# A decoder step on one Trainium2 core: one written order for projections, prompt attention and cached attention

## The reference

```python
x = x + 0.5 * swiglu_ffn(x, ffn1)                      # 1024 -> 2 x 2816 -> 1024
u, q, k, v, qm = split(rmsnorm(x) @ w_in)              # 256 | 512 | 512 | 512 | 256
y_pool = pool_mixer(u)                                 # windows 2, 4, 8, 16; 64x64 maps
q, k   = rotary(rmsnorm(q)), rotary(rmsnorm(k))        # 8 heads x 64
y_moba = moba_attention(q, k_all, v_all)               # prompt: causal in one block of 256
                                                       # sample: 3 of 4 past blocks + own key
y_mem  = mem_attention(rmsnorm(qm), mk, mv)            # 4 heads, 256 memory tokens
x = x + concat(y_pool, y_moba, y_mem) @ w_out
x = x + 0.5 * swiglu_ffn(x, ffn2)
```

## Time and profile before

| | us |
|---|---|
| three runs: median (lowest to highest) | 693.55 (693.41 to 695.11) |
| the profiled execution, its own time | 694.32 |
| its span, first to last instruction | 692.5 |
| PE busy, share of the span | 631.7, 91% |
| DVE busy | 383.8, 55% |
| ACT busy | 281.2, 41% |
| POOL busy | 21.3, 3% |
| mean granted clock of TensorE | 0.956 |

### The profile page before, as it was taken

One profiled execution on the slowest core, in us unless ns is written; L12 is line 12 of the kernel. 1 busy time (PEld: TensorE's weight loads), 2 busy tenths in 40 slices (PEclk: granted clock), 3 DMA queues, 4 the chain that ended last, 5 costly groups with the idle time before them and its releaser, 6 DMA issues.

```text
span 692.5 us, 13430 instructions
## 1 busy us (share of the span) xinstructions
PE 631.7 (91%) x5076; PEld 570.1 (82%) x5076; DVE 383.8 (55%) x648; ACT 281.2 (41%) x448; POOL 21.3 (3%) x25
## 2 busy tenths in 40 slices
PE   6799999999999799988995677699899999999997
PEld 4799999998999676666773455479799999999997
DVE  4567777776544556356336323224776766775443
ACT  5633453336333434242335322433634443334331
POOL 1000000000000100000000220000400000000000
PEclk9989999999999999999998857799999999999999
DMA  9967767855874315655745658515455565556531
GB/s 286 256 197 237 228 184 233 239 184 203 284 238 171 106 45 167 215 183 183 254 167 196 208 183 276 166 48 167 128 154 165 178 180 168 168 180 224 178 115 63
DMA packets 132700, 128.18 MB, mean 185 GB/s; under 512 B 6648, under 2 KB 103815, under 8 KB 132655
## 3 DMA queue, kind: packets, MB, share of 16 engines
q1 hardware_dynamic: 132375, 127.60, 58.0%
q10 hardware_dynamic: 288, 0.08, 0.1%
HBM read 124.95 MB, written 2.83 MB: 185 GB/s over the span
## 4 chain that ended last, share of the span: by engine, by line
PE 60%; DVE 16%; ACT 10%; issue 8%; SPq 3%; POOL 1%; DMA 1%; DVEq 1%; ACTq 0%; POOLq 0%
PE banks L1170 16%; PE banks L1171 16%; PE banks L1172 15%; PE banks L1178 6%; ACT w_hi L546 4%; DVE w_lo L839 4%; PE banks L1510 2%; DVE h_tmp L876 1%; PE banks L1273 1%; DVE h_tmp L879 1%; ACT kv L566 1%; DVE sg L871 1%; POOL kv L528 1%; PE banks L1460 1%; SPq L358 1%
## 5 line engine op out<-in xcount | busy, mean ns | idle before, releaser
L839 DVE TENSOR_TENSOR w_lo<-raw,w_hi 128x1024 fp32r<-128x1024 f32 x160 | 196.1, 1232 | 147.0 <-ACT w_hi L546 145.9
L1170 PE MATMUL banks<-x_hi,w_hi 128*128 128x264 f32 x768 | 222.3, 289 | 10.6 <-DVE h_tmp L876 7.6
L1171 PE MATMUL banks<-x_lo,w_hi 128*128 128x264 f32 x768 | 220.5, 287 | 0.0
L1172 PE MATMUL banks<-x_hi,w_lo 128*128 128x264 f32 x768 | 220.2, 287 | 0.0
L546 ACT ACTIVATE w_hi<-raw 128x1024 fp32r<-128x1024 f32 x160 | 164.6, 1051 | 82.8 <-PE banks L1172 80.2
L1170 PEld LDWEIGHTS banks<-x_hi,w_hi 128*128 128x128 f32 x768 | 147.6, 192 | 12.6 <-DVE w_lo L839 9.7
L1171 PEld LDWEIGHTS banks<-x_lo,w_hi 128*128 128x128 f32 x768 | 147.8, 192 | 0.0
L1172 PEld LDWEIGHTS banks<-x_hi,w_lo 128*128 128x128 f32 x768 | 146.9, 191 | 0.0
L1170 PE MATMUL banks<-h_hi,w_hi 128*128 (+1 forms) x352 | 100.2, 285 | 0.8 <-DVE h_tmp L876 0.7
L1172 PE MATMUL banks<-h_hi,w_lo 128*128 (+1 forms) x352 | 100.2, 285 | 0.0
L1171 PE MATMUL banks<-h_lo,w_hi 128*128 (+1 forms) x352 | 100.0, 284 | 0.0
(11 more groups left out here) (233 smaller groups left out, 558.2 us busy)
## 6 DMA issues: line engine op xcount, KB each, us to landing
raw<-in_ffn_w_in SPq DMA_DIRECT2D x88, 512.0 KB, 3.9
raw<-in_ffn_w_out SPq DMA_DIRECT2D x44, 512.0 KB, 3.3
kv<-in_cache_k SPq DMA_DIRECT2D x64, 256.0 KB, 3.5
kv<-in_cache_v SPq DMA_DIRECT2D x64, 256.0 KB, 4.2
raw<-in_w_in SPq DMA_DIRECT2D x12, 512.0 KB, 3.1
raw<-in_w_out SPq DMA_DIRECT2D x8, 512.0 KB, 5.6
raw<-in_mem_w_kv SPq DMA_DIRECT2D x4, 512.0 KB, 3.2
raw<-in_w_in SPq DMA_DIRECT2D x8, 256.0 KB, 3.7
```

The costliest lines, as they stand in the source:

```text
L839: vec.tensor_tensor(w_lo[:, n % RING, :], raw[:, n % RING, :], w_hi[:, n % RING, :].bitcast(F32), ALU.subtract).then_inc(lo_ready, 1)
L1170: pe.matmul(out, lhs[0], rhs[0], start=start, stop=False)
L1171: pe.matmul(out, lhs[0], rhs[1], start=False, stop=False)
L1172: return pe.matmul(out, lhs[1], rhs[0], start=False, stop=stop)
```

## The change: what it does

It puts the whole stage between the feed-forwards into one list, `steps()`, that all engines follow. In it:

1. The column sums come after the sample parts of units 0 and 1; units 2 and 3 follow them.
2. The cached keys are transposed in rounds 1 to 4 and 6 to 9, eight pages a round (`K_PAGES_AT`), one or two pages behind each part; the logits follow in rounds 2 to 5 and 7 to 10, behind the second part (`LOGITS_AT`). Rounds 10 to 15 have no keys.
3. The norms follow rounds 3 and 5 (prompt queries), 7 and 8 (keys); the cached softmax `A` begins behind rounds 10 and 11 and ends in rounds 14 and 15.
4. The prompt attention goes by single heads (12 units in place of 6 pairs), with `unit_of(u)` giving pair, partitions, lane and the unit that used the bank before. Units 0 to 4 all use lane 0 (banks 0 and 1), from unit 5 on odd units use lane 1 (banks 4 and 5). Scores and value product of a unit share one bank. Units 0 to 3 lie between the parts of rounds 12 to 15. HX is now called PV.
5. After round 15 two units at a time go with one V between; the memory queries, the pooling and the norms of u and qm (5 and 6) lie among them. ACT's function table, loaded for Exp once before, is loaded for Exp ahead of `A`, for Sqrt ahead of norm 5, and again for Exp ahead of unit 4.
6. `MIX`: the first four units of the output projection for six of the eight output tiles come ahead of V 6 and V 7; the other two tiles of these units (banks 2 and 3, which V uses) follow the last Y.
7. The multiplication of the probabilities is a `tensor_scalar` in place of a `tensor_tensor` with a broadcast operand. `qb`, `rows` and the transposed probabilities lie at other addresses.
8. SP: loads of keys 5 to 7 and of the values are issued earlier, `w_out` units behind rounds 8 to 15; the page numbers of sequences 4 to 7 are read during the second half of feed-forward 1 and held in registers (`HELD`), those of 2 and 3 are read at the load.

```diff
-HELD = 6
+HELD = (0, 1, 4, 5, 6, 7)
-KV_STREAM = ([("k", b) for b in range(NS)] + [("v", b) for b in range(3)] + [("mk", 0), ("v", 3), ("mv", 0)] +
-             [("v", b) for b in range(4, NS)])
+KV_STREAM = ([("k", b) for b in range(NS)] + [("v", b) for b in range(3)] + [("mk", 0)] +
+             [("v", b) for b in range(3, 6)] + [("mv", 0), ("v", 6), ("v", 7)])
...
+K_PAGES_AT = {1: 0, 2: 1, 3: 2, 4: 3, 6: 4, 7: 5, 8: 6, 9: 7}
+LOGITS_AT = {2: 0, 3: 1, 4: 2, 5: 3, 7: 4, 8: 5, 9: 6, 10: 7}
...
+            return u // 2, slice(HD * (u % 2), HD * (u % 2) + HD), 0 if u < 4 else u % 2, (u - 1 if u < 5 else u - 2) if u != 5 else None
...
+            after = {1: [("QT", 0)], 3: [("NQ", 2), ("NV", 2), ("ND", 2)], 4: [("T", 5)], 5: [("NS", 2)], 6: [("T", 0)],
+                     7: [("T", 1), ("NQ", 3), ("NV", 3), ("ND", 3), ("NS", 3), ("NQ", 4), ("NV", 4), ("ND", 4)],
+                     8: [("NS", 4), ("OWN", 0)], 9: [("OWN", 1)], 10: [("T", 2), ("A", 0)], 11: [("T", 3), ("A", 1)]}
+            among = {12: [("HA", 0), None, None, None, ("HB", 0), None, None],
+                     13: [("PV", 0), None, ("HA", 1), None, None, None, ("HB", 1)],
+                     14: [None, None, ("PV", 1), ("HA", 2), ("A", 2), None, ("HB", 2)],
+                     15: [None, None, ("PV", 2), ("HA", 3), ("A", 3), None, ("HB", 3)]}
+            for r in range(16):
+                pages = [PAGES * K_PAGES_AT[r] + t for t in range(PAGES)] if r in K_PAGES_AT else []
+                parts = [(r, tt, kk) for tt in range(1 if r < 4 else 0, 3) for kk in range(2)]
+                for idx, part in enumerate(parts):
+                    if r in among and among[r][idx]:
+                        yield among[r][idx]
+                    yield "P", part
+                    if r % 4 == 3 and part[2] == 1:
+                        yield "E", (r // 4, part[1])
+                    if idx == 1 and r in LOGITS_AT:
+                        yield "K", LOGITS_AT[r]
+                    share = 2 if len(parts) == 4 or idx % 3 == 0 else 1
+                    for g in pages[:share]:
+                        yield "G", g
+                    pages = pages[share:]
+                if r in among and among[r][6]:
+                    yield among[r][6]
+                yield "W", r + 4
+                yield from after.get(r, ())
+            yield from [("V", 0), ("PV", 3), ("X", 0), ("POOL", 0), ("NQ", 5), ("NV", 5), ("NQ", 6), ("NV", 6), ("ND", 5), ("ND", 6),
+                        ("HA", 4), ("HA", 5), ("NS", 5), ("V", 1), ("HB", 4), ("L", 0), ("POOL", 1), ("HB", 5), ("NS", 6), ("L", 1),
+                        ("PV", 4), ("PV", 5), ("HA", 6), ("HA", 7), ("V", 2), ("L", 2), ("HB", 6), ("HB", 7), ("T", 4), ("L", 3),
+                        ("PV", 6), ("PV", 7), ("HA", 8), ("HA", 9), ("V", 3), ("HB", 8), ("HB", 9), ("M", 0), ("PV", 8), ("PV", 9),
+                        ("HA", 10), ("HA", 11), ("Y", 0), ("V", 4), ("M", 1), ("HB", 10), ("HB", 11), ("M", 2), ("PV", 10), ("PV", 11),
+                        ("V", 5), ("V", "mem"), ("Y", 1), ("CAT", 0), ("MIX", 0), ("V", 6), ("V", 7), ("Y", 2), ("CAT", 1)]
...
+            for what, k in steps():
+                if what == "P":
+                    project(*k)
+                elif what == "MIX":
+                    pe.wait_ge(ys_ready, 4)
+                    for j in range(4):
+                        pe.wait_ge(lo_ready, U_MIX + j + 1)
+                        pe.wait_ge(cat_lo, j + 1)
+                        for m in M_ORDER[:6]:
+                            three(bank[m][:, 0:N], weights((U_MIX + j) % RING, m * P, (m + 1) * P), mixed[j], j == 0, False)
...
+            for m in M_ORDER[6:]:
+                if m == M_ORDER[6]:
+                    pe.wait_ge(ys_ready, 6)
+                for j in range(4):
+                    mm = three(bank[m][:, 0:N], weights((U_MIX + j) % RING, m * P, (m + 1) * P), mixed[j], j == 0, False)
+                    if m == M_ORDER[7]:
+                        mm.then_inc(w_used, 1)
```

More of the change, by code:

```diff
@@ new lines, in _ @@
+            for what, k in steps():
+                if what == "W":
+                    split(U_WIN + k)
+                elif what == "G" and k % 2 == 0:
+                    key_evac(k)
+                elif what == "E":
+                    evac(k[0], [k[1]])
+                elif what == "T":
+                    turned([k])
+                elif what == "NQ":
+                    act.wait_ge(proj_evac, heads[k][3])
+                    head_squares(k, heads[k][0])
+                elif what == "ND":
+                    head_sd(k, heads[k][1], heads[k][2])
+                elif what == "X":
+                    act.wait_ge(proj_evac, 10)
+                    act.activation(ext[0:NS, :], us[:, 0:POOL], ACT.Copy).then_inc(ext_ready, 1)
@@ L1425, in _ @@
+                    out = bank[SC_BANKS[lane]]
                     for t in range(2):
                         n = keys_of(k, t)
[L1427 to L1430 removed]
+                        mm = pe.matmul(out[:, t * NP:t * NP + n], q_[r, hp, t * P:(t + 1) * P], k_[r, hp, 0:n], start=True, stop=not masked)
@@ L1462, in _ @@
+                        q0 = P if kt and k < MH else 0
+                        mm = pe.matmul(bank[SC_BANKS[lane]][r, q0:NP], v_, probT_pair[lane][:, kt * NP:kt * NP + NP - q0],
+                                       start=(kt == 0), stop=(kt == 1))
                     mm.then_inc(pv_done, 1)
@@ L1464, in _ @@
                     queries(k)
-                elif what == "A" and k == 1:
+                elif what == "A" and k == 2:
                     pe.wait_ge(s_exp, BLOCKS)
```

400 lines of the change are left out of this document (169 added, 231 removed).

## The result

The change made the kernel slower: 705.37 us (median of four runs, 702.67 to 707.61) against 694.33 for the kernel before beside it (693.41 to 698.82); the ratio is 1.0144, 95% interval 1.0084 to 1.0205. I had predicted 687.3 and a range of 675 to 697. The profiled execution took 702.67, the shortest of the four, with a span of 700.9; the 8.4 us by which its span grew lie between the feed-forwards. PE is busy for 642.1 us (631.7 before), DVE for 385.8 and ACT for 288.9.

What follows compares the result with a forecast made beforehand. PE was taken as the bound, losing time to late key-page copies and low clock. Start 9.9, rounds 133.9, tail 79.2, clock 7.5 and projection 17.0 gave 247.5 against 253.7, 6.2 less: 687.3 us, range 675 to 697.

Steps and rivals of the forecast that it cites:

- Step 1: Start: column sums fill PE's wait for `w_lo`, so the rounds begin at 241.9, 1.0 us earlier.
- Step 2: Rounds: a part and another bank's page between two pages of one bank take the 0.75 us lost a round to nothing.
- Step 3: Rounds 1, 6, 8, 9: norms ahead of page copies on DVE open holes of 2.2, 4.0, 2.8, 3.3; 12.3 us together.
- Step 4: Rounds 12 to 15: four heads at 1.65 us, half a pair each; 7.4 us more work and 2.9 of waits.
- Step 5: Rounds: holes lower PE's clock in two spells of 1.9 us, 3.8 charged; rounds 133.9 against 124.8.
- Step 6: Tail after round 15: 79.2 us at full clock, with PE's waits for other engines, plus 7.5 for the clock.
- that rival: Table loads on ACT cost more than their row: a drain behind two loads adds 2.8 us, 690; chance 0.03.
- Step 7: Second part of the output projection: 17.0 us against 23.4, with a 2.4 us wait for unit 4's split.
- Clock stays down: Rounds 6 to 10, tail and `MIX`: holes close together keep the clock low; 709 us, or 698 at half; chance 0.15.
- the likeliest case: The prediction's own forecast: the stretch between the feed-forwards 6.2 us shorter, median 687.3 us; chance 0.51.

Runs made afterwards that it cites:

- e4: Changed kernel with only the 24 column-sum matmuls put back behind the sample parts of all four units: 705.85 us, ratio 1.0153.
- e12: Best version (norms and DVE reductions moved, `MIX` in one piece; 675.9 us) with a round's eight key pages in one piece behind its parts: 690.81 us.
- e8: Changed kernel with norms and DVE reductions moved (684.32 us), its four heads taken from rounds 12 to 15 into the tail: 684.55 us.
- e13: Best version (norms and DVE reductions moved, `MIX` in one piece; 675.90 us), four heads taken from rounds 12 to 15 into the tail: 678.27 us.
- e3: Changed kernel with 15 needless matmuls ahead of the page PE waits 4.05 us for in round 6: 703.53 us, ratio 1.0129.
- e15: Changed kernel with only DVE's memory-query reductions moved behind what PE waits for in the tail: 695.41 us, ratio 1.0008.
- e14: Changed kernel with only `MIX` put back in one piece behind the last value product: 699.37 us, ratio 1.0048.

## Why the prediction was wrong

The steps that failed by size are 4 (what a head costs PE), 5 (the clock in the rounds) and 6 (the tail); step 1 took off a microsecond that was not there, and step 7 priced the two pieces too low. The path through the rounds (steps 2 and 3) was as forecast.

**Step 1, the start: failed.** I took 1.0 us off; the rounds began 0.7 later, and e4 shows no gain either way. POOL was done 0.6 later than I had it, the sums took 3.3 and not 2.6, at a clock of 0.82 in the mean, and the sample parts behind them 5.3 and not 4.8, at 0.50.

**Step 2, the weave: right in the main.** Rounds 2 and 3 take 8.4 and 8.3 us, priced at 8.25; e12 loses 14.9 us without the weave. "Goes to nothing" was not quite so: once holes and clock are taken off, some 2 us of rounds 0 to 11 are left over my prices, up to 0.4 a round, for which I have no test.

**Step 3, the holes: right in place, short in sum.** 1.5, 4.05, 3.9 and 3.1 us stood in rounds 1, 6, 8 and 9, forecast 2.2, 4.0, 2.8 and 3.3. The one in round 8 waits for ACT, not DVE: ACT's root (`sd_h`) stands behind DVE's sum of squares, and the page copy behind the root:

```profile
321.25 0.22 ACT L629 ACTIVATE sd_h<-var_h 128x16 f32<-128x16 f32 x1 [3.11 <-DVE var_h L921]
321.37 0.58 ACT L589 ACTIVATE kv<-banks 128x512 f32<-128x512 f32 x1
```

One of 0.6 us in round 4 I had not: 13.2 in all for 12.3.

**Step 4, the heads: the price of a unit failed.** I took a unit as half a pair, 1.65 us. Round 15 shows what it takes, values, scores and transposes, each up to the start of the next row:

```profile
379.80 0.86 PE L1459 MATMUL banks<-probT_odd,vp 128*64 128x256 f32 x4
380.59 0.50 PE L1167 MATMUL banks<-w_hi,x_hi 128*128 128x512 f32 x1
...
381.48 0.48 PE L1437 MATMUL banks<-kT,qT 64*128 64x128 f32 x2
...
382.72 0.48 PE L1167 MATMUL banks<-w_hi,x_hi 128*128 128x512 f32 x1
...
385.56 0.55 PE L1175 MATMUL banks<-ident,prob_pair 128*128 128x128 f32 x3
386.04 1.96 PE L1510 MATMUL banks<-kv,p_cols 128*32 128x128 f32 x64
```

That is 0.79, 1.24 and 0.48, 2.5 us, since the two heads of a pair had run side by side; four units, one without values, are 9.2 us and not 6.2. Waits were fewer than charged (1.8 for 2.9), and the lower clock behind that wait took some 1.6. Rounds 12 to 15 are 4.8 over: 3.0 for the units, 1.6 for the clock, less 1.1 for the waits, and 1.3 that I can't assign. And e8 and e13 show that even so the place of the heads makes no difference.

**Step 5, the clock: right in kind, too low.** I charged 3.8 in two spells. Round 6 took 14.9 us for 12.3 of work and hole by my prices, round 8 15.2 for 13.5, so 2.6 and 1.7 went to the clock; the wait ahead of unit 0 cost some 1.6 more: 5.9. In the start the lower clock cost about 1 more than I had. That a hole brings the clock down e3 shows. How much of it one hole brings down, no charge per hole can say: behind the 3.1 us of round 9 it was 1.00 in three traces of the same rounds and 0.51 in a fourth.

**Step 6, the tail: 3.5 over.** The waits stood where I put them: 2.9, 3.1, 5.1 us ahead of units 4, 5 and 6, none of 2.3 ahead of unit 8, and 3.0 ahead of Y 0, for 2.9, 4.1, 6.1, 2.3 and 2.7. These are 14.1 us for 18.1, so some 7.5 us must lie in PE's own work at the lower clock and in single heads, beyond the 7.5 charged for the clock; the two are not told apart here. I had seen the order that makes them, reductions ahead of multiplications, and priced it as given; e15 shows that it costs 10 us. Of the unknown prices, the two multiplications of a head took 0.55 (taken 0.5), and the instruction behind a table load started at 398.57 after a load that began at 397.27 and took 1.28: no drain, and that rival is out.

**Step 7, the output projection: priced too low.** I set 17.0 against 23.4, with the 8.8 of the early piece in the tail's sum. Put together, my own numbers had the two pieces 2.4 above one, by one wait of 2.4, and nothing in the sum was won by it. e14 has them 6.0 above. That wait took 1.37; the one of 1.70 ahead of the early piece I had at nothing. Nothing was covered, since V 6, V 7 and Y 2 are dense without it but for the same 0.81 and 0.89.

**The rivals.** The slower side was the right one, by none of them as written. Clock stays down: 698 to 709 holds the time, but its mechanism is wrong, the clock came back within 4 to 6 us of the end of each hole in the rounds. That the range of a rival holds the time is luck. What happened is the likeliest case with every stage too low: 1.7, 3.7, 4.8, 3.5 and 0.8. In the rounds the separate sum for the clock was 2.1 short (5.9 for 3.8) and the price of the units 3.0; the shares in the tail stay open. The range of 675 to 697 left 10 us on the slower side; five misses that all went the same way were more.

## What to carry to other kernels

- Weaving pays only as far as the in-order queues of the copying engines allow. Before any order is priced, write down for each engine the longest stretch of work ahead of something that PE waits for; put such stretches where PE asks nothing (rounds without pages or behind what PE waits for: 12 us here), and never a step that waits for a slow engine (POOL) ahead of one that PE waits for (10 us).
- Work moved into a dense stage costs its full PE time there, and gains only what it had cost in waits. Ask what idle time the moved piece fills at its new place; if none, two pieces mean two more waits (3.1 us of the 6 that `MIX` in two pieces cost here).
- Half of a pair is not half of the price where the two run side by side.
